# Expert inputs gathered by TensorE from rows on chip instead of row loads, gate and up weights in blocks of 128 rows, three of eight expert visits at 64 places

## The reference

```
def moe_swiglu(h, router, wg, wu, wd):            # h: rows x 1024, after RMSNorm with gain
    probs = softmax(h @ router)                    # 8 experts
    vals, idx = top_k(probs, 2)                    # each row goes to two experts
    combine = one_hot weights, normalised over the two
    for e in range(8):
        out += combine[:, e] * ((silu(h @ wg[e]) * (h @ wu[e])) @ wd[e])   # 1024 -> 3584 -> 1024
```

## Time and profile before

| | before |
|---|---|
| device time, median of 3 | 1543.45 us |
| the profiled execution's own time | 1543.34 us |
| its span, first to last instruction | 1541.5 us |
| mean granted TensorE clock | 0.996 of full speed |
| PE busy | 1511.2 us (98%) |
| DVE, ACT busy | 643.9 us (42%), 404.6 us (26%) |
| moved by DMA | 515.88 MB |
| visit 0 begins, visit 7 begins (PE) | 682.63 us, 1443.33 us |
| last expert matmul ends (PE) | 1526.7 us |

### The profile page before, as it was taken

One profiled execution on the slowest core, in us unless ns is written; L12 is line 12 of the kernel. 1 busy time (PEld: TensorE's weight loads), 2 busy tenths in 40 slices (PEclk: granted clock), 3 DMA queues, 4 the chain that ended last, 5 costly groups with the idle time before them and its releaser, 6 DMA issues.

```text
span 1541.5 us, 31601 instructions
## 1 busy us (share of the span) xinstructions
PE 1511.2 (98%) x14136; PEld 903.7 (59%) x14136; DVE 643.9 (42%) x1025; ACT 404.6 (26%) x613; POOL 86.6 (6%) x118
## 2 busy tenths in 40 slices
PE   9999999999999999999999999999999999999986
PEld 7888889999999999864333333333333333333322
DVE  7566878677656897551301301301311312112034
ACT  4444666544455547530000010010010000000001
POOL 1122221000000011010000000000000000000001
PEclk9999999999999999999999999999999999999998
DMA  9687786688656545569999999999999999999995
GB/s 373 223 287 268 258 291 216 201 275 280 223 179 209 199 164 196 233 234 418 426 408 427 426 425 427 424 419 429 405 424 430 395 423 427 401 427 416 423 427 249
DMA packets 136937, 515.88 MB, mean 335 GB/s; under 512 B 6488, under 2 KB 58912, under 8 KB 128480
## 3 DMA queue, kind: packets, MB, share of 16 engines
q1 hardware_dynamic: 116672, 450.03, 73.7%
q0 software_dynamic: 15968, 57.97, 10.2%
q10 hardware_dynamic: 4160, 5.84, 1.1%
HBM read 473.48 MB, written 40.34 MB: 333 GB/s over the span
## 4 chain that ended last, share of the span: by engine, by line
issue 53%; PE 37%; DVE 3%; ACT 1%; DMA 1%; POOL 0%; POOLq 0%; ACTq 0%; DVEq 0%
PE ps L2020 35%; DMA ring<-y_scr,expert_arena 1%; PE ps L2233 1%; DVE ring L1458 0%; POOL y_scr L962 0%; ACT ring_low_parts L1019 0%; DVE expert_arena L1969 0%; PE ps L2360 0%; DVE expert_arena L1986 0%; DVE ring_low_parts L1408 0%; DVE expert_arena L1976 0%; DVE expert_arena L1894 0%; ACT arena L1196 0%; PE ps L2481 0%; DVE arena L1748 0%
## 5 line engine op out<-in xcount | busy, mean ns | idle before, releaser
L2020 PE MATMUL ps<-ring,expert_x_turned 128*32 128x448 f32 x5152 | 488.8, 539 | 1.6 <-issue 0.8
L2020 PEld LDWEIGHTS ps<-ring,expert_x_turned 128*32 128x32 f32 x5152 | 169.5, 110 | 318.1 <-issue 316.2
L2020 PE MATMUL ps<-normed_high,ring_low_parts 128*128 128x264 f32 x1344 | 267.2, 290 | 0.4 <-DVE normed_low L1392 0.4
L2020 PE MATMUL ps<-ring,expert_hidden_turned 128*32 128x512 f32 x2360 | 257.4, 595 | 6.0 <-DMA ring<-in_moe_w_down 6.0
L1408 DVE TENSOR_TENSOR ring_low_parts<-ring,ring_low_parts 128x1024 fp32r<-128x1024 f32 (+3 forms) x184 | 209.1, 1142 | 84.6 <-ACT ring_low_parts L1019 84.2
L1019 ACT CAST ring_low_parts<-ring 128x1024 fp32r<-128x1024 f32 (+3 forms) x184 | 180.8, 983 | 222.9 <-PE ps L2020 214.3
L1947 DVE TENSOR_TENSOR expert_arena<-expert_arena,ps 128x1344 f32<-128x1344 f32 (+1 forms) x16 | 23.9, 1496 | 481.8 <-PE ps L2020 481.8
L2020 PEld LDWEIGHTS ps<-normed_high,ring_low_parts 128*128 128x128 f32 x1344 | 214.9, 189 | 5.4 <-issue 4.2
L2020 PEld LDWEIGHTS ps<-ring,expert_hidden_turned 128*32 128x32 f32 x2360 | 76.8, 110 | 184.0 <-issue 174.4
L2020 PE MATMUL ps<-normed_low,ring_low_parts 128*128 128x264 f32 x640 | 159.3, 284 | 0.0
L2020 PE MATMUL ps<-h_parts,ring_low_parts 128*128 128x264 f32 x1056 | 129.6, 285 | 0.0
(11 more groups left out here) (294 smaller groups left out, 1157.0 us busy)
## 6 DMA issues: line engine op xcount, KB each, us to landing
ring<-in_moe_w_gate SPq DMA_DIRECT2D x64, 1792.0 KB, 12.0
ring<-in_moe_w_down SPq DMA_DIRECT2D x47, 2048.0 KB, 13.6
ring<-in_moe_w_up SPq DMA_DIRECT2D x48, 1792.0 KB, 12.2
expert_piece_slot<-in_moe_w_up SPq DMA_DIRECT2D x16, 1792.0 KB, 13.0
ring<-in_ret_w_in SPq DMA_DIRECT2D x8, 2048.0 KB, 11.1
ring<-in_state_retention POOLq DMA_DIRECT2D x32, 512.0 KB, 6.6
out_ret_s<-ring POOLq DMA_DIRECT2D x32, 512.0 KB, 4.0
ring<-in_hg_w_in SPq DMA_DIRECT2D x8, 2048.0 KB, 8.0
```

Of the source, the lines that this page charges most:

```text
L2020: return nc.tensor.matmul(out, lhsT, rhs, start=first, stop=last)
```

## The change

`C_FEW = 64` and `FEW = (7, 4, 1)`: visits 7, 4 and 1 (in words counted from one: 8, 5 and 2) now have 64 places in two groups, and the three experts with the fewest rows are swapped into them. The scatter to DRAM, the row loads, the normed rows and the transposes of rows are gone. Instead PE forms the turned rows of the next visit behind piece 17 of every visit: 24 matmuls with a 128 x 128 block of `x_tok` as weights and the 96 or 64 columns of `gsel` streamed; DVE builds that selection beforehand and multiplies the result by the gain. As `xe` then has feature 128k + p in partition p, gate and up weights are loaded as `"e (k p) n -> p e k n"`: a piece is two blocks of 128 neighbouring rows, of which each partition takes half a row (7168 bytes) as before. The diff, cut to its core:

```diff
-C_LAST = 64
-GROUPS = [TG] * (NE - 1) + [C_LAST // 32]
+C_FEW = 64
+FEW = (7, 4, 1)
+GROUPS = [C_FEW // 32 if v in FEW else TG for v in range(NE)]
...
-        moe_g = ins["moe_w_gate"][0].rearrange("e (p k) n -> p e k n", p=P)
-        moe_u = ins["moe_w_up"][0].rearrange("e (p k) n -> p e k n", p=P)
+        moe_g = ins["moe_w_gate"][0].rearrange("e (k p) n -> p e k n", p=P)
+        moe_u = ins["moe_w_up"][0].rearrange("e (k p) n -> p e k n", p=P)
...
-        X_AT, X_AT_LAST = 12, 2
+        GATHER_BEHIND = 17
```

On SP and POOL:

```diff
-            def load_rows(i):
-                sp.dma_start(x_row, y_scr[bass.ds(i * C, P), :]).then_inc(x_row_in, 16)
...
-                    if t == (X_AT if v < NE - 1 else X_AT_LAST):
-                        sp.wait_ge(xe_ok, i + 1)
-                        load_rows(i + 2)
...
-            for t in range(3):
-                m = P if t < 2 else NS
-                for w in range(2):
-                    pool.indirect_dma_start(y_scr[:, :], bass.IndirectOffsetOnAxis(ap=rowi[0:m, w, t:t + 1], axis=0),
-                                            h_tok[0:m, t, :], None).then_inc(x_scattered, 16)
```

On DVE, ahead of the loop and (the last 15 lines) in it:

```diff
+            def selection(v, numbers):
+
+                for t in range(3):
+                    m = P if t < 2 else NS
+                    i = V.tensor_scalar(gsel[0:m, t, 0:32 * GROUPS[v]], numbers[0:m, 0:32 * GROUPS[v]],
+                                        rank_at[0:m, t, v:v + 1], rstd_tok[0:m, t:t + 1], ALU.is_equal, ALU.mult)
+                i.then_inc(sel_ok, 1)
...
+            link(V.tensor_scalar(rounds_f[:, 4:5], fewest[:, len(FEW) - 1:len(FEW)], -float(C_FEW), 1.0, ALU.is_lt, ALU.add))
...
+                for n, v in enumerate(FEW):
+                    link(V.tensor_scalar(swap_at, expert_at, fewest_expert[:, n:n + 1], None, ALU.is_equal))
...
+                    link(V.tensor_copy(by_visit[:, :, v], swap_of))
...
+            def take_expert_x(v, q, o):
+
+                w = 32 * GROUPS[v]
+                return V.tensor_tensor(xe[:, 4 * q:4 * q + 4, 0:w], o[:, 0:4 * w].rearrange("p (k s) -> p k s", k=4),
+                                       vec[:, GAIN3 + 4 * q:GAIN3 + 4 * q + 4].unsqueeze(2).to_broadcast([P, 4, w]), ALU.mult)
...
-                    dve.wait_ge(x_row_in, i * 16 + 16)
-                    for t in range(GROUPS[(e + 1) % NE]):
-                        for c in range(4):
-                            j = V.transpose(xe[32 * c:32 * c + 32, :, 32 * t:32 * t + 32],
-                                            x_row[32 * t:32 * t + 32, 256 * c:256 * c + 256].rearrange("p (f b) -> p b f", b=KD))
-                    j.then_inc(xe_ok, 1)
+                        if h == 0:
+                            selection((e + 1) % NE, places)
+                            dve.wait_ge(sel_ok, i + 2)
+                            rank_of_further_round((e + 1) % NE)
...
+                    for q in range(2):
+                        dve.wait_ge(x_full, i * 2 + (q + 1))
+                        j = take_expert_x((e + 1) % NE, q, ps[:, 6 + q, :])
+                    j.then_inc(xe_ok, 1)
```

On PE:

```diff
+            def gather_x(q, o, w):
+
+                for k in range(4 * q, 4 * q + 4):
+                    for s in range(3):
+                        m = P if s < 2 else NS
+                        i = mm(o[:, w * (k % 4):w * (k % 4) + w],
+                               x_tok[0:m, s, P * k:P * k + P], gsel[0:m, s, 0:w],
+                               s == 0, s == 2)
+                return i
...
-            keep_busy(("hw", 5), 512, 384)
+            keep_busy(("hw", 5), 128)
...
+                        if t == GATHER_BEHIND:
+                            if e == 0:
+                                pe.wait_ge(last_sel_ok, r * TL + (1 + TL))
+                            pe.wait_ge(sel_ok, n + 2)
+                            for q in range(2):
+                                gather_x(q, ps[:, 6 + q, :], 32 * GROUPS[(e + 1) % NE]).then_inc(x_full, 1)
```

More of the change, by code:

```diff
@@ L491, in hybrid_step @@
         marks = part(earena, RB + 418, 32)
-        last_sel = part(sel_mem, 0, TG, NT)
+        last_sel = part(sel_mem, 0, TL, NT)
         pos_wide = part(earena, 8512, 3, P)
@@ L1836, in _, with rank_of_further_round @@
             rk = bank(("rk", 0))[:, 0:32].rearrange("p (a e) -> p a e", a=4)
[L1837 to L1843, removed]
+            link(V.scalar_tensor_tensor(out=rank_at, in0=rk[:, 0:3, :], scalar=1.0, in1=mm_, op0=ALU.add, op1=ALU.mult))
+            def selection(v, numbers):
[4 more added lines that the diff above has]
+                i.then_inc(sel_ok, 1)
+            def rank_of_further_round(v):
+                V.tensor_scalar(rank_at[:, :, v], rank_at[:, :, v], -32.0 * GROUPS[v], None, ALU.add)
+            selection(0, cc("slot"))
             V.reduce_max(rounds_f[:, 0:1], rk[:, 3, :], AX.X)
-            V.tensor_reduce(rounds_f[:, 3:4], rk[:, 3, 1:NE], AX.X, ALU.min)
-            frees(V.tensor_copy(counts, rk[:, 3, :]), ("rk", 0))
+            frees(V.tensor_scalar(fewest_in[:, 1:NE], rk[:, 3, 1:NE], -1.0, None, ALU.mult), ("rk", 0))
             freed(dve, ("rk", 0))
@@ new lines, in rows_of_tokens @@
+            def rows_of_tokens():
+                V.tensor_tensor(r1, rank_at.unsqueeze(1).to_broadcast([P, 2, 3, 8]), oab, ALU.mult)
+                link(V.tensor_tensor(swap_tmp[:, 0:6], by_visit[:, 4:10], cc("exp8").unsqueeze(1).to_broadcast([P, 6, 8]),
+                                     ALU.mult))
+                V.reduce_sum(va, r1, AX.X)
+                link(V.reduce_sum(visit_of.rearrange("p w t -> p (w t)"), swap_tmp[:, 0:6], AX.X))
+                link(V.tensor_scalar(few_off, visit_of, float(FEW[0]), float(C - C_FEW), ALU.is_equal, ALU.mult))
+                for v in FEW[1:]:
+                    link(V.tensor_scalar(vt, visit_of, float(v), float(C - C_FEW), ALU.is_equal, ALU.mult))
+                    link(V.tensor_tensor(few_off, few_off, vt, ALU.add))
+                link(V.tensor_scalar(rowf, visit_of, float(C), float(C - 1), ALU.mult, ALU.add))
@@ L1882, in rows_of_tokens @@
                 V.tensor_tensor(rowf, rowf, va, ALU.add)
[L1883 to L1886, removed]
+                V.tensor_scalar(vt, va, float(2 * C + 1), None, ALU.is_ge)
+                link(V.tensor_tensor(va, va, few_off, ALU.add))
@@ L1887, in rows_of_tokens @@
+                link(V.scalar_tensor_tensor(out=vt, in0=va, scalar=float(C + 1), in1=vt, op0=ALU.is_ge, op1=ALU.add))
+                link(V.scalar_tensor_tensor(out=vt, in0=few_off, scalar=float((NE - 1) * C), in1=vt,
                                             op0=ALU.add, op1=ALU.mult))
[L1888 to L1902, removed]
-            order_of_visits()
[L1904 to L1910, removed]
@@ L1912, in _ @@
+            dve.wait_ge(rows_in, 16)
+            for q in range(2):
+                filled(dve, ("first", q))
+                i = take_expert_x(0, q, bank(("first", q)))
+                frees(i, ("first", q))
+            freed(dve, ("first", 1))
+            dve.sem_inc(xe_ok, 1)
+            order_of_visits()
             rows_of_tokens()
[L1913 to L1917, removed]
+            rank_of_further_round(0)
@@ L2610, in _ @@
             pe.wait_ge(last_sel_ok, rounds * TL + 1)
+            mm(ps[0:32, last_bank[2], 0:1], ident[:, 0:32], ident[:, 0:1])
+            pe.wait_ge(xe_ok, last + 2)
             mm(ps[0:32, last_bank[2], 0:1], ident[:, 0:32], ident[:, 0:1])
```

99 lines of the change are left out of this document (40 added, 59 removed).

## The result

| | before | after |
|---|---|---|
| device time, median | 1542.98 us | 1585.76 us (1584.68 to 1587.81, 4 runs) |
| ratio to before | | 1.0279, 95% interval 1.0261 to 1.0297 |
| span of the profiled execution | 1541.5 us | 1586.0 us |
| mean granted TensorE clock | 0.996 | 0.969 |

A forecast was written before the change was run, and what follows sets the result against it. The prediction took PE and DMA as balanced within some per cent, with DMA deciding after the change; 17.1 us less without dips or 9.4 with them gave 13.2, so 1543.34 - 13.2 = 1530.1, predicted 1530.5 us, range 1523 to 1543.

The forecast's parts named there:

- What the gathers take from PE: Each visit's gather on PE: 48 records at 0.115 us, 5.5 us, plus 0.3 for the change of form, 5.8 us.
- the 8.1 from which PE decides: Gather time in us from which PE, not DMA, sets the pace over three visits; slower than before from 10.3 us.
- the clock falls in the narrow visits: Rival: PE's clock drops in visits 1, 4 and 7; if it held, 154 us late, 1685 us; chance 0.02.
- The upper bound: Gather on PE without any overlap: 48 x 0.273 = 13.1 us, putting the kernel's end at 1565 us.
- The walk: Step through visits 0 to 7 and the ring of pieces, taking the later of PE and DMA; PE ends at 1509.6.
- PE stays the bound: Rival: longer gathers make PE decide, from 8.1 us each; 0.12 that it decides, 0.06 that the kernel gets slower.
- The walk where DMA decides: Forecast case: DMA sets the starts of visits 2 and 5; dips from none to all, 1524 to 1537 us; chance 0.62.
- The layout costs nothing: Gate and up loads: rate assumed unchanged; the rival, worse loading, had 0.10, half of it slower; 5% would be 1550.
- the dips: Stretches of a visit at 415 to 423 GB/s instead of 426, costing 7.7 us in all; cause left open.
- the middle between 17.1 us less without dips and 9.4 with them: Gain at PE's end of the visits: 13.2 us taken, as dips in the new layout could not be known.
- The one that was weighed: Rule that loops waiting for DMA may be throttled at every piece: visits 1, 4 and 7 at half speed, 144 us each.
- the chance of "slower": Chance that the changed kernel takes longer than before, stated as 0.11, beside faster 0.80 and same 0.09.

The follow-up runs named there:

- in threes: The changed kernel with each gather's 24 matmuls spread in groups of three behind pieces 12 to 15 and 17 to 20: 1552.83 us, ratio 1.0075.
- the halves of visit 1: The changed kernel with each gather cut into two stretches of 12 matmuls, behind pieces 17 and 19: 1573.42 us, ratio 1.0196.
- the row form: The changed kernel with every gather using the selection as weights and x_tok streamed, DVE's product and turn behind, old weight layout: 1534.45 us, ratio 0.9956.
- the early start: The row form with three narrow visits and its first gather handed to DVE in two parts: 1531.88 us, ratio 0.9941.
- the row form with one narrow visit: The row form with only visit 7 narrow, instead of visits 1, 4 and 7: 1576.99 us, ratio 1.0232.
- no gathers: The changed kernel without the eight gathers inside the visits, the one ahead of visit 0 kept: 1534.14 us, ratio 0.9954.
- with no gathers: The early start kernel without the eight gathers in the visits, which then use stale rows: 1528.62 us, ratio 0.9916.

## Why the prediction was wrong

**The step that failed** is "What the gathers take from PE": "I take 0.115: 5.5 us, and 0.3 for the change of form at both sides, 5.8 us". Measured are 8.9 to 11.3 us for the gather and up to 3 us more in the pieces behind it. The term was too small by two parts that can be told apart:
- *The price at full clock.* The 0.114 us came from the 128-wide records. Those are transposes: L2351 issues eight instructions and leaves eight records, while a float32 matmul leaves two. They are not the same work. The matmuls of the ranks gave 0.120 at 24 columns. A gather at the upper level of the clock takes 0.167 us a record, in threes as in the halves of visit 1, which would make 8.0 us of one stretch, about the 8.1 from which PE decides; no run shows a whole gather at that level. In threes, at the upper level throughout, it cost 9.1 us, and that is over it.
- *The clock.* The case "the clock falls in the narrow visits" looked for it where PE waits. It falls where PE is busy with gathers, in all visits, for which the prediction had no term. The same matmuls in threes, with the clock up, end 33 us earlier: that is the clock's share of the 52 us that the gathers cost, as far as spreading changes nothing else; the threes also let slots come free between them, and I did not part these two.

**The upper bound** was 13.1 us a gather, and its price to the visit came true, though by the clock and not by a missing overlap: 121.0 - 108.5 = 12.5 us in visit 2, 13.9 in visit 3. Its time, 1565, was still 21 us short. The walk predicted PE's end at 1509.6 and it came at 1572.0. The 62 us are: 4.8 from the start (688.2 for 683.4: the first gather too runs at the lower clock), 6.6 in visit 0 (123.8 for 117.2), 15.1 in visits 2 and 3, 12.1 in 5 and 6, and 8.5 + 6.8 + 8.5 in visits 1, 4 and 7. The last were taken as the larger of PE's and DMA's time. In truth PE first waits for pieces (9 us in visit 1, up to piece 17) and then gathers for 9.6 us: the two add up in part, since the wait stands ahead of the gather. The start and this sum were in neither the case "PE stays the bound" nor its price.

**What held.** The narrow visits: worth 42.5 us in the row form (35 to 45 had been set down) and 50 in the changed kernel. Their PE work of 72.1 us holds for pieces in a row; behind waits each gate or up piece takes 3.21 us, and visit 4 without gathers shows 77.0 us busy. The walk where DMA decides: in the row form visit 2 starts at 888.4 (886.2 predicted), visit 5 at 1203.8 (1199.1), and the kernel with the early start takes 1531.9, where the prediction said 1530.5. DMA's time for a visit was 315.4 / 3 = 105.1 us, not 104.3: the rate was the 426 GB/s assumed, but the queues moved 134.6 MB in visits 2 to 4 of the row form, 44.9 MB each, where 44.43 had been counted. The layout costs nothing, as assumed.

**What held for another reason.** "So by the waits PE is the bound. But the stretches of one visit show both at once": the DMA share of 1.01 was read as a full DMA. In the row form with one narrow visit PE decides, DMA has slack, and still its share is 0.97 to 1.00 at 395 to 413 GB/s. And the dips of the earlier trace rows are gone in every stretch where DMA always has pieces to load, in the old layout (row form) as in the new (no gathers). The prediction's own 44.96 MB over PE's 108.2 us are 415.5 GB/s, and the last stretches of the earlier trace rows show 415 and 417. That fits dips that are DMA's slack behind a bound PE and no loss of rate; it was not tested by itself. So the middle between 17.1 us less without dips and 9.4 with them answers to nothing: where DMA decides there are no dips, and the walk without them (17.1 us less, 1526.2) is the one that applies. The kernel with the early start takes 5.7 us more than that. PE's last expert matmul ends at 1514.0 instead of 1509.6, of which 2.6 us are there by visit 5 (1201.7 for 1199.1, three visits of 105.1 us instead of 104.3), and the tail behind it takes 16.1 us where it took 14.8. Measured were 9.8 us less with the early start and 13.1 with no gathers; that the forecast of 1530.5 came near to the first is luck, two errors that cancel.

**Did a rule stand against it?** The one that was weighed (The Trainium skill, TensorE: Matmul & The Clock Gate, HAM oscillation) speaks of waits for DMA that are longer than the work between them. Here the work between the waits, 3.2 to 3.6 us, was the longer part. The narrow visits with waits of about 1.1 to 1.6 us before each piece show 1.00 in the row form, and 0.98 in the changed kernel without gathers, where one wait of 2.0 to 2.7 us stands in each. So by these traces it does not bite at each piece, and the prediction was right to give it little; what brought the clock down was another thing.

**A sum.** By the prediction's own list the chance of "slower" is 0.06 + 0.05 + 0.02 = 0.13, not 0.11.

## What to carry to other kernels

Price a matmul by rows of the same kind: a transpose, a float32 matmul and a matmul in four column groups differ in records and in weight loads, and a price per record carries over to none of the others. On a PE that is the bound, keep small matmuls with full 128x128 weights in short groups between wide ones, or turn them around so that the narrow operand is the weights: the same selection cost 4.7 us instead of 9 to 11, and the clock stayed up. Leave out work for a round that does not come: the gather in the last visit stood right before the end. Where PE and DMA alternate as the bound behind a ring of limited depth, neither visit's saving can be added to the other's: add a small walk through the ring, and put each wait and each piece of work in it in its true order.

## What was not expected of the hardware

- The granted clock of TensorE fell to 1.2 GHz while PE was busy in every row. In the gather of visit 0 (774.02) it fell at about 777.9, 3.9 us in, and was low for some 10 us, until 788; in that of visit 1 (877.75) at about 883.8, 6 us in, and low for some 7; in that of visit 3 (1109.65) it fell within 3 us. Six such records at a time between wide matmuls never brought it down in the visits; 24 did in seven of eight visits, in four of them at both halves, and in visit 1 at neither.
- In the visits, gathers of 64 columns took 8.9 to 11.2 us and those of 96 columns 9.6 to 11.3. At the upper level of the clock a half of 24 records took 777.93 - 774.13 = 3.80 us with 64 columns and 4.01 us with 96. A third fewer columns saved a twentieth: the columns hardly set the pace, which suggests that the load of the weights does; no run parts the two.
- Two waits of 2.51 us (before visit 0 of the row form, and in the earlier trace rows) were each followed by a stretch at the lower level, which cost 1.7 us. A wait of 2.0 us in visit 1 of the changed kernel without gathers was followed by one too, one of 2.41 us in visit 7 of the same kernel was not, and waits of 1.1 to 1.6 us between pieces were not.
- A matmul of this kind with 8 rows of weights is no cheaper: in the changed kernel's gathers those records last as long as those with 128 rows (389 and 361 ns on average in visit 2):

```profile
L2005 PE MATMUL ps<-expert_arena 128*128 128x96 f32 x32 | 7.2, 361 | 0.0
L2005 PE MATMUL ps<-expert_arena 8*128 8x96 f32 x16 | 4.8, 389 | 0.0
```
